# Expert tiles in Strassen pairs: 92 of 128 before the spread, and the gates stored from ScalarE's queue

## The chip, the cores and the metric

The program runs on one core of one Trainium2 chip. The time is device microseconds (us) of one execution. The kernel before took 5091.68 us (median of three runs, 5091.26 to 5094.24). The engines are TensorE (PE in the profile; PEld is its weight load), VectorE (DVE), ScalarE (ACT), GpSimd (POOL) and SyncE (SP), which in this kernel only issues transfers.

## The reference, cut to what matters

One decoder layer: token mixers, cross-attention, and a product-key retrieval of experts. Only the last is touched by the change. With 1024 tokens of width 1024, eight heads, and 128 x 128 experts of one neuron each:

```python
def peer_ffn(h, w_pq, sub_keys, u_emb, v_emb):
    q = (h @ w_pq).reshape(b, s, 8, 2, 128)                 # the queries
    sc = jnp.einsum('bshpc,pnc->bshpn', q, sub_keys)
    top_v, top_i = lax.top_k(sc, 16)                        # 16 of 128, twice
    cand = (top_v[..., 0, :, None] + top_v[..., 1, None, :]).reshape(b, s, 8, 256)
    best_v, best_i = lax.top_k(cand, 16)                    # 16 of 256
    expert = i1 * 128 + i2                                  # from top_i and best_i
    gate = jax.nn.softmax(best_v, axis=-1)
    ...                                                     # by blocks of 128 tokens
        a = jnp.einsum('bthkd,btd->bthk', u_emb[e_blk], h_blk)
        act = (jax.nn.gelu(a) * g_blk)
        return jnp.einsum('bthk,bthkd->btd', act, v_emb[e_blk])
```

The kernel does not gather experts. It computes gelu(u · h) for all 16,384 experts and all tokens, spreads the 128 gates of a token over a row of 16,384, and multiplies densely.

## The kernel before, in words

Matrices are multiplied in `three_pass` (L145): each float32 operand is split into a high part, rounded by ScalarE's copy to the fp32r type, and a low part, the remainder, and a product of a 128 x 128 weight chunk with 512 tokens is three matmuls (high·high, high·low, low·high; L149 to L151). A tile is 128 rows of weights: 8 chunks of the width times two halves of 512 tokens times three passes, so 48 matmuls of 512 columns.

The stages follow each other with a barrier of all engines between them: mixers, merge, cross-attention, then

- **select** (`select_phase`, L1412). The normalised input h, [128, 8, 1024], is made on VectorE and split into `hhi` and `hlo`. A loop over the 8 heads computes per head two tiles of queries (`queries`, L1549), their scores against the keys (`scores`, L1562), and six tiles of gelu(u·h) (`Experts1`, L1339): 48 of the 128 expert tiles in all, which give TensorE work while VectorE picks the top 16, twice, of the head before. At the end the selected indices and gates are turned (transposed) on TensorE, copied out, stored to memory (`sel`) and loaded by the next stage.
- **spread** (`spread_phase`, L1750). The remaining 80 expert tiles, and beside them 64 spread steps of 16 tokens each: VectorE makes a one-hot matrix of the first key and one of the second times the gate (L1862, L1871; four instructions of 128x2048 float16 per step, in two buffers), TensorE multiplies them (L1886, 32 matmuls per step), ScalarE copies the four banks to `stage` (L1906). A group of 128 tokens has eight steps and ten tiles: one tile before each step, and two tiles behind the last. `stage` then holds 8 MB, and SyncE stores it as two transfers of 4 MB (L1820), each issued between two of the tile's own transfers: the load of an expert tile (`uraw`, L1371) and the store of a gelu tile (`gelu_u`, L1376). ScalarE begins the next group's first step only when both have landed.
- **expert** multiplies gelu and gates and runs the second expert matrix, 128 tiles of it, then the final norm.

What one engine does for a tile: SyncE loads 512 KB; ScalarE makes the high part (L1383), GpSimd the low part (L1387); TensorE runs the 48 matmuls; ScalarE applies gelu from each of two banks (L1404); SyncE stores. TensorE waits in `product` for the gelu of the tile before in the same bank. The order on every engine is the order in the code; nothing is reordered.

Of the kernel before, what the change touches and what calls it, by code (L numbers as in the profile page):

```python
# [23 lines left out]
SELECT_TILES = 48  # L24
SB_HD = 64
XH = 4
PH = 8
# [16 lines left out]
class Phase:  # L44
# [9 lines left out]
    def sb(self, name, shape, dt=F32):  # L54
        return self.tensors.enter_context(self.nc.sbuf_tensor(f"{self.tag}_{name}", shape, dt))

# [1282 lines left out]
class Experts1:  # L1339
# [8 lines left out]
    def __init__(self, nc, tensors):  # L1348
        sb = lambda name, shape, dt=F32: tensors.enter_context(nc.sbuf_tensor(name, shape, dt))
        self.nc = nc  # L1350
        self.hhi, self.hlo = sb("hhi", [P, NC, T], F32R), sb("hlo", [P, NC, T], F32R)
        self.raw = sb("uraw", [P, 2, NC, P])
        self.hi, self.lo = sb("uhi", [P, 2, NC, P], F32R), sb("ulo", [P, 2, NC, P], F32R)
        self.out = sb("ugelu", [P, 2, T])

    def begin(self, m, u_stream, a_out):

        self.u_stream, self.a_out = u_stream, a_out
        self.ps = m.ps("a", [P, 2, H])
        self.loaded = [m.sem(f"u_loaded{s}") for s in range(2)]  # L1360
        self.hi_made, self.lo_made = m.sem("uhi_made"), m.sem("ulo_made")
        self.done = m.sem("a_done")
        self.gelu = m.sem("a_gelu", start=2)
        self.stored = [m.sem(f"a_stored{s}", start=1) for s in range(2)]
# [3 lines left out]
    def load(self, sync, tile0, n, slot, first=False):  # L1368
        if not first:
            sync.wait_ge(self.lo_made, n - 1)  # L1370
        sync.dma_start(self.raw[:, slot], self.u_stream[ds(n + tile0, 1)].rearrange("a p c n -> (a p) c n")  # L1371
                       ).then_inc(self.loaded[slot], 16)

    def store(self, sync, tile0, n, slot):
        sync.wait_ge(self.gelu, n * 2 + 4)
        sync.dma_start(self.a_out[ds(n + tile0, 1)].rearrange("a p t -> (a p) t"), self.out[:, slot]  # L1376
                       ).then_inc(self.stored[slot], 16)

    def split_high(self, act, n, m, slot, first=False):
        act.wait_ge(self.loaded[slot], m * 16 + 16)  # L1380
        if not first:
            act.wait_ge(self.done, n * 2 - 2)
        self.nc.scalar.activation(self.hi[:, slot], self.raw[:, slot], ACT.Copy).then_inc(self.hi_made, 1)  # L1383

    def split_low(self, pool, n, slot):
        pool.wait_ge(self.hi_made, n + 1)
        self.nc.gpsimd.tensor_tensor(self.lo[:, slot], self.raw[:, slot], self.hi[:, slot].bitcast(F32), ALU.subtract  # L1387
                                     ).then_inc(self.lo_made, 1)

    def product(self, pe, n, slot):  # L1390
        pe.wait_ge(self.hi_made, n + 1)
        pe.wait_ge(self.lo_made, n + 1)
        for h in range(2):
            pe.wait_ge(self.gelu, n * 2 + (h + 1))
            mm = three_pass(self.nc, self.ps[:, h], [(self.hi[:, slot, k], self.lo[:, slot, k],
                                                      self.hhi[:, k, h * H:h * H + H], self.hlo[:, k, h * H:h * H + H])
                                                     for k in range(NC)])
            mm.then_inc(self.done, 1)

    def activate(self, act, n, m, slot):  # L1400
        act.wait_ge(self.stored[slot], m * 16 + 1)
        for h in range(2):
            act.wait_ge(self.done, n * 2 + (h + 1))
            self.nc.scalar.activation(self.out[:, slot, h * H:h * H + H], self.ps[:, h], ACT.Gelu_apprx_tanh  # L1404
                                      ).then_inc(self.gelu, 1)

    def finish(self, sync, n):
        for s in range(2):
            sync.wait_ge(self.stored[s], n // 2 * 16 + 1)


def select_phase(nc, ex, x_in, gain, keysT, wstream, u_stream, a_out, sel_out):  # L1412


# [4 lines left out]
    with Phase(nc, "select") as m:  # L1419
        K = TOPK  # L1420
        xT = m.sb("xT", [P, NC, T])

        room = xT[:].rearrange("p c t -> p (c t)")
        sc = room[:, 0:2048].rearrange("p (c t n) -> p c t n", c=2, t=NT)
        sc2 = room[:, 2048:4096].rearrange("p (c t n) -> p c t n", c=2, t=NT)
        cand = room[:, 4096:6144].rearrange("p (t n) -> p t n", t=NT)
        cand2 = room[:, 6144:8192].rearrange("p (t n) -> p t n", t=NT)
        sq = ex.out
        norm = Rsqrt(m, "norm", T)
# [3 lines left out]
        w_raw = m.sb("wraw", [P, 2, NC, P])  # L1433
        w_hi, w_lo = m.sb("whi", [P, 2, NC, P], F32R), m.sb("wlo", [P, 2, NC, P], F32R)
        qT = m.sb("qT", [P, 2, T])
# [8 lines left out]
        hit = m.sb("hit", [P, NT, K, K])  # L1444
# [3 lines left out]
        res = m.sb("res", [P, 3, NT, PH, K])  # L1448
        resT = room[:, 0:3 * T].rearrange("p (r t) -> p r t", r=3)

        gemm = m.ps("gemm", [P, 2, H])
        scps = m.ps("scps", [P, 2, NT, KEYS])

# [3 lines left out]
        squares = SumSquares(m, sq, norm.inv, gemm)  # L1457
        h_made, hhi_made, hlo_made = m.sem("h_made"), m.sem("hhi_made"), m.sem("hlo_made")
        w_loaded = [m.sem(f"w_loaded{c}") for c in range(2)]
        whi_made, wlo_made = m.sem("whi_made"), m.sem("wlo_made")  # L1460
        group_done = m.sem("group_done")
        evicted = [m.sem(f"evicted{b}") for b in range(2)]
        scored = m.sem("scored", start=1)
        sc_made = m.sem("sc_made", start=1)
# [10 lines left out]
        turn_done, turn_read = m.sem("turn_done"), m.sem("turn_read")  # L1475
        held = m.sem("held")
        stored = m.sem("stored")
        ex.begin(m, u_stream, a_out)
        NX = SELECT_TILES // PH
        block = m.block()  # L1480

# [6 lines left out]

        @block.sync
        def _(sync):  # L1490
            for i in range(4):
                sync.dma_start(xT[:, 2 * i:2 * i + 2, :], x_in[:, 2 * i:2 * i + 2, :]).then_inc(x_loaded[i], 16)
            sync.dma_start(g_sb[:], gain).then_inc(c_loaded, 16)
            sync.dma_start(keys[:], keysT).then_inc(c_loaded, 16)
            for c in range(2):
                sync.dma_start(w_raw[:, c], wstream[c]).then_inc(w_loaded[c], 16)
            for s in range(2):
                ex.load(sync, 0, s, s, first=True)

            def body(hd, first, last):  # L1500
                for i in range(NX):
                    if i in (0, 1) and not last:
                        sync.wait_ge(wlo_made, hd * 2 + (i + 1))
                        sync.dma_start(w_raw[:, i], wstream[ds(hd * 2 + (2 + i), 1)].rearrange("a p c n -> (a p) c n")
                                       ).then_inc(w_loaded[i], 16)
                    if not (last and i >= NX - 2):
# [244 lines left out]

# [491 lines left out]
```

## Time and profile before

| | |
|---|---|
| median of three runs | 5091.68 us |
| the profiled execution, whole | 5093.29 us |
| its span, first to last instruction | 5091.6 us |
| PE busy | 4756.0 us, 93% |
| DVE, ACT, POOL busy | 2591.5, 1628.5, 1247.9 us |
| mean granted clock of TensorE | 0.962 |

The sum of the prediction is made against the profiled execution, which is 1.6 us above the median. A matmul's own duration in the rows (0.39 us for 512 columns) overlaps the next one's; the pace is read from the distance between starts. Granted clock 1.0 is 2.4 GHz, 0.5 is 1.2 GHz. DMA instructions stand under SPq (or ACTq): their duration is the time the queue's engine spent on issuing, not the transfer.

### The profile page before, as it was taken

The page shows a single profiled execution, that of the slowest core. Times are in us where ns is not written, and L with a number is a line of the kernel's source. Part 1 is how long each engine was busy: PE and PEld are TensorE (multiplying, and loading weights), DVE is VectorE, ACT ScalarE, POOL GpSimd, SP SyncE. Part 2 cuts the span into 40 slices and gives each one's busy share as a digit, 9 for nine tenths or more (in the row PEclk, how much of TensorE's full clock was granted, in tenths as well). Part 3 has the DMA queues.
Part 4 walks back from the last instruction along what each step waited for, and adds up shares of the span by engine and source line. Part 5 has one row for each costly group of instructions (what it writes and reads, how often), then busy time and mean ns, then how long its engine had stood idle before and what let it go on. Part 6 is the DMA issues. An engine that isn't in the chain of part 4 may idle for free. (4 is left out here: it accounts for less than half of the span.)

```text
span 5091.6 us, 64130 instructions
## 1 busy us (share of the span) xinstructions
PE 4756.0 (93%) x22416; PEld 3785.5 (74%) x22416; DVE 2591.5 (51%) x4079; ACT 1628.5 (32%) x2585; POOL 1247.9 (25%) x754
## 2 busy tenths in 40 slices
PE   6999999976988979999989999999799999999998
PEld 5666666644767758888868888888588888888886
DVE  3777777784514235646554444444344444444445
ACT  3555555553413322222223333333211111111111
POOL 1444434431114112212212111211122222222221
PEclk8999999978989979999999999999899999999999
DMA  2111111104432122222224444444644444344341
GB/s 76 38 42 47 46 47 46 38 17 157 153 120 83 56 102 79 83 74 86 79 84 156 148 148 151 154 148 148 227 165 148 144 148 141 138 144 148 140 148 67
DMA packets 260924, 555.78 MB, mean 109 GB/s; under 512 B 15664, under 2 KB 146992, under 8 KB 258608
## 3 DMA queue, kind: packets, MB, share of 16 engines
q1 hardware_dynamic: 260784, 554.01, 31.9%
q8 instruction: 76, 1.25, 0.1%
q14 instruction: 64, 0.52, 0.0%
HBM read 384.60 MB, written 169.35 MB: 109 GB/s over the span
## 5 line engine op out<-in xcount | busy, mean ns | idle before, releaser
L149 PE MATMUL expert_o<-expert_ahi,expert_vhi 128*128 128x512 f32 x2048 | 798.9, 390 | 35.0 <-POOL expert_vlo L2007 30.1
L151 PE MATMUL expert_o<-expert_ahi,expert_vlo 128*128 128x512 f32 x2048 | 797.9, 390 | 0.0
L150 PE MATMUL expert_o<-expert_alo,expert_vhi 128*128 128x512 f32 x2048 | 797.9, 390 | 0.0
L2071 DVE TENSOR_TENSOR expert_acc<-expert_acc,expert_o 128x512 f32<-128x512 f32 x496 | 341.1, 688 | 710.2 <-PE expert_o L151 705.5
L1387 POOL TENSOR_TENSOR ulo<-uraw,uhi 128x1024 fp32r<-128x1024 f32 x128 | 311.7, 2436 | 1373.6 <-ACT uhi L1383 1373.6
L2007 POOL TENSOR_TENSOR expert_vlo<-expert_vraw,expert_vhi 128x1024 fp32r<-128x1024 f32 x128 | 323.1, 2525 | 1053.1 <-ACT expert_vhi L2025 1053.1
L149 PE MATMUL spread_a<-hhi,uhi 128*128 128x512 f32 x1280 | 505.5, 395 | 15.1 <-POOL ulo L1387 15.1
L151 PE MATMUL spread_a<-hhi,ulo 128*128 128x512 f32 x1280 | 499.5, 390 | 0.0
L150 PE MATMUL spread_a<-hlo,uhi 128*128 128x512 f32 x1280 | 498.6, 390 | 0.0
L149 PEld LDWEIGHTS expert_o<-expert_ahi,expert_vhi 128*128 128x128 f32 x2048 | 385.1, 188 | 117.2 <-issue 36.4
L1862 DVE TENSOR_TENSOR spread_one<-spread_iota,spread_parts 128x2048 f16<-128x2048 f16 x64 | 184.0, 2875 | 527.5 <-PE spread_g L1886 526.8
L150 PEld LDWEIGHTS expert_o<-expert_alo,expert_vhi 128*128 128x128 f32 x2048 | 385.2, 188 | 80.1 <-issue 0.2
L151 PEld LDWEIGHTS expert_o<-expert_ahi,expert_vlo 128*128 128x128 f32 x2048 | 385.1, 188 | 80.2
L149 PE MATMUL mix_gemm<-mix_hhi,mix_w_hi 128*128 128x512 f32 x896 | 374.6, 418 | 20.5 <-POOL mix_w_lo L179 13.5
L2031 ACT ACTIVATE expert_ahi<-expert_act 128x1024 fp32r<-128x1024 f32 x128 | 135.8, 1061 | 738.7 <-DVE expert_act L2061 732.1
L550 DVE SCALAR_TENSOR_TENSOR mix_room<-mix_u,mix_cwj,mix_room 128x1024 f32<-128x1024 f32 x240 | 361.3, 1506 | 6.1 <-DVE mix_u L522 3.2
L150 PE MATMUL mix_gemm<-mix_hlo,mix_w_hi 128*128 128x512 f32 x896 | 363.5, 406 | 0.0
L151 PE MATMUL mix_gemm<-mix_hhi,mix_w_lo 128*128 128x512 f32 x896 | 363.0, 405 | 0.0
L149 PE MATMUL select_a<-hhi,uhi 128*128 128x512 f32 x768 | 299.5, 390 | 0.0
L151 PE MATMUL select_a<-hhi,ulo 128*128 128x512 f32 x768 | 298.9, 389 | 0.0
L150 PE MATMUL select_a<-hlo,uhi 128*128 128x512 f32 x768 | 298.8, 389 | 0.0
L1404 ACT ACTIVATE ugelu<-spread_a 128x512 f32<-128x512 f32 x160 | 95.8, 599 | 616.8 <-PE spread_a L151 616.8
(289 smaller groups left out, 8596.9 us busy)
## 6 DMA issues: line engine op xcount, KB each, us to landing
uraw<-in_peer_u SPq DMA_DIRECT2D x128, 512.0 KB, 4.1
gelu_u<-ugelu SPq DMA_DIRECT2D x128, 512.0 KB, 2.9
gates<-spread_stage SPq DMA_DIRECT2D x16, 4096.0 KB, 17.3
expert_act<-gelu_u SPq DMA_DIRECT2D x128, 512.0 KB, 3.6
expert_graw<-gates SPq DMA_DIRECT2D x128, 512.0 KB, 4.4
expert_vraw<-in_peer_v SPq DMA_DIRECT2D x128, 512.0 KB, 6.6
mix_w_raw<-in_w_mix SPq DMA_DIRECT2D x56, 512.0 KB, 3.7
xattn_w_raw<-in_w_cross SPq DMA_DIRECT2D x32, 512.0 KB, 3.6
```

What stands on the lines that cost most here:

```text
L149: nc.tensor.matmul(out, whi, xhi, start=(first and i == 0), stop=False)
L150: nc.tensor.matmul(out, whi, xlo, start=False, stop=False)
L151: mm = nc.tensor.matmul(out, wlo, xhi, start=False, stop=(last and i == len(terms) - 1))
L550: nc.vector.scalar_tensor_tensor(out=ybuf[:, par], in0=u[:, par, t:t + T], scalar=cwj[:, t:t + 1], in1=ybuf[:, par], op0=ALU.mult, op1=ALU ...
L1387: self.nc.gpsimd.tensor_tensor(self.lo[:, slot], self.raw[:, slot], self.hi[:, slot].bitcast(F32), ALU.subtract).then_inc(self.lo_made, 1)
L1404: self.nc.scalar.activation(self.out[:, slot, h * H:h * H + H], self.ps[:, h], ACT.Gelu_apprx_tanh).then_inc(self.gelu, 1)
L1862: return nc.vector.tensor_tensor(pairwise(dst), keys, twice(row, n), ALU.is_equal)
L2007: return eng.tensor_tensor(low, raw, high.bitcast(F32), ALU.subtract)
L2031: nc.scalar.activation(ahi[:, par, e], act[:, e], ACT.Copy).then_inc(ahi_made, 1)
L2071: nc.vector.tensor_tensor(acc[:, k, h * H:h * H + H], acc[:, k, h * H:h * H + H], ops[:, d, h], ALU.add).then_inc(added, 1)
```

## The change

In the stages before select, and in expert, nothing is changed but line numbers (moved by six in the shared helpers).

**Pairs.** In select, two tiles go together as a pair (256 rows x 1024 of the width, times 1024 tokens), cut into 2 x 2 blocks on every side, and are multiplied by Strassen's scheme in Winograd's form: seven products of half size instead of eight. A half product is 4 chunks x 3 passes = 12 matmuls of 512 columns, a pair 84. The eight query pairs and 46 pairs of expert tiles (92 tiles) make 54 pairs. GpSimd makes four sums of 128x512 per pair (L1414 on) and the low parts of seven blocks; ScalarE the high parts; the token side's sums T are made once, by VectorE, when the stage begins. The products come out in four banks; ScalarE copies the first one, VectorE adds the others in seven instructions of 128x512 into the buffer `out`, and ScalarE applies gelu there, in place.

```diff
+    def sums(self, pool, n, m, s):
+        a, g = self.raw[:, s], self.nc.gpsimd
+        pool.wait_ge(self.loaded[s], m * 16 + 16)
+        g.tensor_tensor(a[:, 2], a[:, 0], a[:, 2], ALU.subtract).then_inc(self.sum_made, 1)
+            pool.wait_ge(self.done, n * self.NP - 4)
+        g.tensor_tensor(self.s2[:], a[:, 3], a[:, 2], ALU.subtract).then_inc(self.sum_made, 1)
+        g.tensor_tensor(self.s14[:, s, 0], a[:, 0], self.s2[:], ALU.add).then_inc(self.sum_made, 1)
+        g.tensor_tensor(self.s14[:, s, 1], a[:, 1], self.s2[:], ALU.subtract).then_inc(self.sum_made, 1)
...
+    def product(self, pe, n, s, j, made=None):
+        if j != 1:
+            pe.wait_ge(self.lo_made, n * 4 + (group + 1))
+        if j == 0 and not first:
+            pe.wait_ge(self.added, n * self.NP - 3)
+        if j == 1 and not first:
+            pe.wait_ge(self.added, n * self.NP - 1)
+        if j == 2 and not first:
+            pe.wait_ge(self.added, n * self.NP)
...
+            mm = three_pass(self.nc, self.ps[:, bank], [(high[:, kp], low[:, kp], b_hi[:, k], b_lo[:, k])],
```

**Select's VectorE work.** The top-16 search of a head was one block. It is cut into pieces of one to eight instructions that stand between the additions of six pairs. The turned indices go straight from the banks into `parts` (kept in the shared buffer `front`), so `sel` is neither stored nor loaded, and the turning is done inside the last five pairs. On VectorE, third pair of a head, where the old `select_xT<-select_top` is the candidate sum (L1700) and the new one `front<-select_top` (L1888); `front<-front,select_products` are the pair's additions. Before:

```order
L1697 MAX_INDEX select_idx<-select_top,select_xT 128x8 x16
L1700 TENSOR_TENSOR select_xT<-select_top 128x256 x8
L1705 CAST select_idxf<-select_idx 128x256
L1709 MAX select_best<-select_xT 128x8 x8
L1712 MAX_INDEX select_bidx<-select_best,select_xT 128x8
```

After:

```order
L1884 MAX_INDEX select_idx<-select_top,front 128x8 x2
L1888 TENSOR_TENSOR front<-select_top 128x256 x3
L1490 TENSOR_TENSOR front<-front,select_products 128x512
L1492 TENSOR_TENSOR front<-front,select_products 128x512
L1888 TENSOR_TENSOR front<-select_top 128x256 x5
L1495 TENSOR_TENSOR front<-front,select_products 128x512
L1979 CAST select_idxf<-select_idx 128x256
```

The eight candidate sums now stand three before and five behind a pair's additions, and the addition at L1495, for which TensorE's next pair waits, stands behind the five.

**Spread.** 36 tiles are left. A group of 128 tokens has four tiles (the last has eight): six half tiles, then the eight steps, with one half tile behind the second and one behind the fourth step; the last group's other eight half tiles come last. VectorE's step buffers are three instead of two. Gelu's output buffer and its stores are by half tile (256 KB). The loops are written out.

```diff
+        def order(tt, half, step):
+            first, between, rest = halves(tt)
+            for n, h in first:
+                half(n, h)
+            for st in range(0, STEPS, 2):
+                step(tt * STEPS + st)
+                step(tt * STEPS + st + 1)
+                for n, h in between[st // 2:st // 2 + 1]:
+                    half(n, h)
...
+    def product(self, pe, n, h):
+        pe.wait_ge(self.lo_made, n + 1)
+        if n:
+            pe.wait_ge(self.gelu, 2 * n + h - 1)
...
+                if n >= 3:
+                    dve.wait_ge(g_done, (n - 2) * NB)
...
-                part = slice(i * KEYS // NS, (i + 1) * KEYS // NS)
-                sync.dma_start(g_out[part].rearrange("a p t -> p a t")[:, :, ds(tt * P, P)], stage[:, part, :]
-                               ).then_inc(stored, 16)
+                if st == STEPS - 1:
+                    act.wait_ge(staged, (n + 1) * NB)
+                    for i in range(NS):
+                        part = slice(i * KEYS // NS, (i + 1) * KEYS // NS)
+                        nc.scalar.dma_start(g_out[part].rearrange("a p t -> p a t")[:, :, tt * P:tt * P + P], stage[:, part, :]
+                                             ).then_inc(stored, 16)
```

`NS` goes from 2 to 4. The store of the gates leaves SyncE's queue. There it stood, behind the eighth step of a group, between a tile's load and store:

```order
L1371 DMA uraw<-in_peer_u 128x1024
L1818 ISA
L1820 ISA
L1820 DMA gates<-spread_stage 128x64x128
L1375 ISA
L1376 ISA
L1376 DMA gelu_u<-ugelu 128x1024
```

It is now on ScalarE, at the end of a group's steps (`spread_stage<-spread_g` are the copies out of the banks, four per step):

```order
L2235 ACTIVATE spread_stage<-spread_g 128x128x4 x8
L2098 ACTIVATE spread_ugelu<-spread_a 128x512
L2078 ACTIVATE spread_uhi<-spread_uraw 128x1024
L2235 ACTIVATE spread_stage<-spread_g 128x128x4 x16
L2241 DMA gates<-spread_stage 128x32x128 x4
L2098 ACTIVATE spread_ugelu<-spread_a 128x512 x2
L2078 ACTIVATE spread_uhi<-spread_uraw 128x1024
```

Four issues of 2 MB each stand ahead of the gelu of the next group's first tile, in ScalarE's own order.

## Rows read from the trace of the kernel before

**Rows 1.** Stages, by window: us, then busy time and count by engine, clock, DMA share, GB/s.
```profile
core 0: us, PE busy (x) PEld busy (x) DVE busy (x) ACT busy (x) POOL busy (x), PEclk, DMA share, GB/s
1878.00:1912.00 34.00, 29.81 (x96) 20.89 (x97) 15.20 (x13) 10.03 (x11) 4.83 (x2) 0.73 0.05 16
1912.00:2623.00 711.00, 708.18 (x3234) 587.36 (x3232) 419.13 (x1711) 170.04 (x225) 146.57 (x60) 1.00 0.23 78
2623.00:2643.40 20.40, 4.84 (x24) 3.81 (x24) 0.29 (x1) 5.70 (x8) 2.81 (x3) 0.59 0.50 197
2643.40:3640.00 996.60, 994.14 (x5888) 829.10 (x5888) 412.14 (x257) 335.88 (x525) 190.80 (x79) 1.00 0.47 147
3640.00:3669.50 29.50, 0.03 (x1) 0.06 (x1) 7.23 (x5) 3.10 (x4) 2.64 (x2) 0.56 0.90 313
```

**Rows 2.** ACT's timeline in select: start, us, instruction, idle before and releaser.
```profile
2233.34 0.60 ACT L1404 ACTIVATE ugelu<-select_a 128x512 f32<-128x512 f32 x1 [4.84 <-PE select_a L151]
...
2244.22 0.60 ACT L1404 ACTIVATE ugelu<-select_a 128x512 f32<-128x512 f32 x1 [4.84 <-PE select_a L151]
```

**Rows 3.** Groups by line and shape, POOL: busy us, mean ns, idle before.
```profile
L1387 POOL TENSOR_TENSOR ulo<-uraw,uhi 128x1024 fp32r<-128x1024 f32 x128 | 311.7, 2436 | 1373.6 <-ACT uhi L1383 1373.6
...
L327 POOL TENSOR_TENSOR mix_sp_lo<-mix_softplus,mix_sp_hi 128x512 fp32r<-128x512 f32 x48 | 61.7, 1285 | 219.8 <-ACT mix_sp_hi L473 218.2
```

**Rows 4.** Timeline of DVE, POOL and PE around the first spread steps.
```profile
2653.15 1.23 DVE L1862 TENSOR_TENSOR spread_one<-spread_iota,spread_parts 128x2048 f16<-128x2048 f16 x1 [0.62 <-DVE spread_parts L1847]
...
2657.93 1.22 DVE L1862 TENSOR_TENSOR spread_one<-spread_iota,spread_parts 128x2048 f16<-128x2048 f16 x1
2657.95 3.45 POOL L1387 TENSOR_TENSOR ulo<-uraw,uhi 128x1024 fp32r<-128x1024 f32 x1 [12.46 <-ACT uhi L1383]
2658.15 1.96 PE L1886 MATMUL spread_g<-spread_gate,spread_one 128*128 128x128 f16 x32 [1.85 <-DVE spread_gate L1871]
...
2659.07 3.42 DVE L1862 TENSOR_TENSOR spread_eq<-spread_iota,spread_parts 128x2048 f16<-128x2048 f16 x1
```

**Rows 5.** Timeline of DVE and POOL at the end of a head in select.
```profile
2061.19 2.29 DVE L1739 TENSOR_TENSOR select_hit<-select_hit,select_idxf 128x2048 f32<-128x2048 f32 x1
2063.28 2.46 POOL L1387 TENSOR_TENSOR ulo<-uraw,uhi 128x1024 fp32r<-128x1024 f32 x1 [8.47 <-ACT uhi L1383]
2063.61 2.29 DVE L1742 TENSOR_REDUCE select_res<-select_hit 128x2048 f32 x1
```

**Rows 6.** One line, expert's additions out of a bank: duration ns, min/median/max.
```profile
L2071 DVE TENSOR_TENSOR expert_acc<-expert_acc,expert_o x496: 675/689/689, 3682.7 to 5027.1; 128x512 f32<-128x512 f32 x166
```

**Rows 7.** SyncE's timeline behind the first group of steps.
```profile
2751.45 0.41 SPq L1820 DMA_DIRECT2D gates<-spread_stage  x1
2761.36 3.34 SPq L1376 DMA_DIRECT2D gelu_u<-ugelu  x1
...
2766.16 1.08 SPq L1820 DMA_DIRECT2D gates<-spread_stage  x1
2772.23 9.36 SPq L1376 DMA_DIRECT2D gelu_u<-ugelu  x1
```

**Rows 8.** The 16 stores of L1820, each 4 MB: issue to landing.
```profile
DMA to landing us min/median/max: 16.0/17.3/19.0
```

**Rows 9.** SyncE's timeline at the end of spread.
```profile
3640.07 8.05 SPq L1376 DMA_DIRECT2D gelu_u<-ugelu  x1
3654.26 0.35 SPq L1981 DMA_DIRECT2D expert_act<-gelu_u  x1
```

**Rows 10.** SyncE's timeline from the end of cross-attention to select.
```profile
1842.17 0.32 SPq L1064 DMA_DIRECT2D x<-xattn_xq  x1
1846.74 2.05 SPq L1492 DMA_DIRECT2D select_xT<-x  x4
```

**Rows 11.** Timeline of SyncE and PE where spread begins.
```profile
2636.07 0.81 SPq L1371 DMA_DIRECT2D uraw<-in_peer_u  x2
...
2643.41 0.79 PE L149 MATMUL spread_a<-hhi,uhi 128*128 128x512 f32 x1 [15.11 <-POOL ulo L1387]
...
2647.25 0.39 PE L149 MATMUL spread_a<-hhi,uhi 128*128 128x512 f32 x1
```

More of the change, by code:

```diff
@@ L1336, in _ @@
                         nc.vector.tensor_tensor(x, x, gemm[:, h], ALU.add).then_inc(bank_read, 1)
[L1339 to L1409, printed above, removed]
@@ L1652, in _ @@
             dve.wait_ge(squares.done, 1)
[L1653 removed]
+            norm.start(nc, dve, [(slice(h * H, h * H + H), pr.ps[:, h]) for h in range(2)], lambda h: sum_read[h])
             norm.finish(nc, dve)
@@ new lines, in spread_phase, with halves @@
+        g_done = m.sem("g_done")
+        staged = m.sem("staged")
+        stored = m.sem("stored")
+        block = m.block()
+        def halves(tt):
+            count = PER if tt < NT - 1 else TILES - PER * (NT - 1)
+            every = [(tt * PER + i // 2, i % 2) for i in range(2 * count)]
+            return every[:FIRST], every[FIRST:FIRST + BETWEEN], every[FIRST + BETWEEN:]
+        def order(tt, half, step):
[7 more added lines that the diff above has]
+                    half(n, h)
+            for n, h in rest:
+                half(n, h)
@@ L1824, in _ @@
-            tiles(sync, step, extra)
-            ex.finish(sync, KEYS - SELECT_TILES)
-            sync.wait_ge(stored, 16 * NS * NT + 1)
+            for n in range(3):
+                ex.load(sync, n)
+            for n in range(TILES):
+                ex.store(sync, SELECT_TILES, n, 0)
+                if n + 3 < TILES:
+                    ex.load(sync, n + 3)
+                ex.store(sync, SELECT_TILES, n, 1)
+            for h in range(2):
+                sync.wait_ge(ex.stored[h], 16 * TILES)
@@ L1885, in step @@
                         for i in range(2):
-                            mm = nc.tensor.matmul(ps[:, bank, x], one1[:, b, t], gate[:, i, b, t], start=(i == 0), stop=(i == 1))
+                            mm = nc.tensor.matmul(ps[:, bank, x], one1[:, b, t], gate[b][:, i, t], start=(i == 0), stop=(i == 1))
                     mm.then_inc(g_done, 1)
-            tiles(pe, step, lambda i, tt, tile, half, b, left: ex.product(pe, tile, b))
+            for tt in range(NT):
+                order(tt, lambda n, h: ex.product(pe, n, h), step)
@@ L1917, in expert_phase @@
+            for tt in range(NT):
+                order(tt, half, step)
 def expert_phase(nc, a_in, x_in, g_in, v_stream, final_gain, out):
```

813 lines of the change are left out of this document (552 added, 261 removed).

## The prediction

> **What bounds the kernel now.** I read the page's busy shares first: PE is busy 93% of the span, no other engine over 51%. Then the windows by stage [rows 1]: in select's steady part PE is busy 708 of 711 us and in spread 994 of 997, both at granted clock 1.00 (2.4 GHz). The time of these stages is the number of matmuls, so a change that takes matmuls away is paid in full as long as nothing else becomes late. The pace comes from ScalarE's timeline: two gelus of the same bank start 10.88 us apart [rows 2], a tile of 48 matmuls, so 0.2267 us per matmul and 5.44 us per half tile. A spread step's 32 matmuls take 1.96 us [rows 4]; as a check, 80 tiles at 10.88 and 64 steps at 1.96 are 996 us [rows 1]. What stands outside: PE idles or crawls for 34 us at select's first tiles, 20 us between select and spread, 29.5 us before expert [rows 1].
>
> **Matmuls removed.** Select and spread have 16 query and 128 expert tiles, 144 x 48 = 6912 matmuls. After: 54 pairs x 84 + 36 x 48 = 6264. 648 fewer, x 0.2267 = **-147 us**. Steps and scores stay.
>
> I follow the new kernel on the clock of the profiled execution.
>
> **Select begins (to 1932).** The first products wait for h as before (1878). Before, the first query pair was through at 1912 [rows 1]. Now products 3 to 6 of the first pair wait for the token sums T: four sums and four low parts of 128x2048 on VectorE, 2.3 us each (as L1739, [rows 5]), 18.6 us behind h. GpSimd, which was idle then, makes sums and low parts at the same time, and where both engines read two operands from SBUF the later one waits for the other's whole instruction: the POOL instruction at 2657.95 took 3.45 instead of 2.4 us (the DVE instruction in flight ended at 2659.1), and the DVE instruction at 2659.07 took 3.42 instead of 1.22, of which 2.3 until POOL's end at 2661.4 [rows 4]. I count five or six such collisions, about 7 us before h is ready and 3 behind. First pair done at about 1932.
>
> **Select runs (to 2988).** A pair is 84 x 0.2267 = 19.04 us on PE. Per pair GpSimd has five instructions of 128x512 (1.285 us) and three of 128x1024 (2.44) [rows 3]: 13.7 us, so it keeps up. VectorE has 419/8 = 52 us of selection per head [rows 1] plus 42 additions of 0.62 to 0.69 us [rows 6]: 80 us in a head's 118, so it keeps up on average too. What can make PE wait is a late addition. PE's third product needs the last addition of the pair before, two products (5.4 us) after its source was done. Laying a head's pieces between the additions with the rows' durations, this slack is used up at one place: the five candidate sums that stand ahead of the third pair's last addition read two SBUF operands while GpSimd works on the next pair; they alternate with its instructions and the addition comes about 1.4 us late. The four 2.3 us instructions of the last pair lose time in the same way, but fit. The reduction does not collide: it began at 2063.61 inside a POOL instruction and took its 2.29 [rows 5]; nor do the additions, with one operand in a bank: 675 to 689 ns through the whole of expert [rows 6]. So 8 x 1.4 = 11 us (bounds 0 and 50: no piece late, or every pair late by about 1). Select's last matmul: 1932 + 53 x 19.04 + 30 for the scores (unchanged) + 5 for turning (4.84, [rows 1]) + 11 = 2988. Before it ended at 2620.
>
> **Select to spread (to 3002).** Before 23 us, with turning, store and reload of the selection. Now the last addition and gelu (1.5 us), a store; from such a store's issue to the next stage's first instruction it is 4.6 us [rows 10], and from that to the first product 7.3 [rows 11]. 14 us.
>
> **Spread.** Work: 36 x 10.88 + 64 x 1.96 = 517 us. Two waits are new.
>
> VectorE: a step costs it 4.8 us (2653.15 to 2657.93, [rows 4]) against PE's 1.96. Before, a tile stood between two steps. Now steps 5 to 8 of a group follow each other, and three are buffered ahead. The fourth is begun when the first is multiplied, and so on; with one half tile behind the second and one behind the fourth step, steps 7 and 8 each come 3 us late (one GpSimd collision among them). **+6 per group, +48**; and 0.6 per group where ScalarE's copies of consecutive steps (4 x 0.51) outlast PE's 1.96: +5. Bounds: 20 and 70.
>
> ScalarE's queue: this is the term that decides. On SyncE, a transfer issued behind 4 MB of 512-byte runs is held: the 4 MB issue itself took 0.41 us, but the next transfer, tried 9.9 us later, was held 3.34 us, until 13.3 us behind the big issue; behind the second it was held 9.36 us, until 15.4 us behind it [rows 7]. The store lands after 16.0 to 19.0 us [rows 8]. So an issue is accepted only when nearly all runs of the one before have been handed on, some 3 us before it lands. SyncE had nothing else to do; ScalarE has. Four issues of 2 MB at the same 290 GB/s (4 MB in 14 us): the second is accepted after about 6, the third 7 later, the fourth 7 later. ScalarE is held about **20 us** and gives no gelu. PE gets through the first tile of the next group (two half tiles, 10.9 us) and then waits for that tile's first gelu. It started 0.9 us before ScalarE's issues, so it waits 0.9 + 20 + 0.5 + 0.6 - 10.9 = 11 us. That is 8 times, as the last group has tiles behind it too: +89. An idle time of this length lowers the clock: behind the 15 us at 2643.41, nine matmuls took 3.84 us instead of 2.04 [rows 11], so +1.7 each, +14. Together **+103**. Bounds: 0, if ScalarE's issues go through at 0.4 us each; and 150, if each is held as long as half of SyncE's second case and the loads on the other queue share the rate (26 us).
>
> Spread ends at 3002 + 517 + 53 + 103 = 3675.
>
> **Before expert.** The gates' last store was issued at 3632 and ended the stage: from the last gelu store at 3640.07 to expert's first transfer were 14.2 us, 8.05 of them held [rows 9]. Now eight half tiles stand behind it, so only the 4.6 us of a barrier [rows 10] are left, and expert starts 5.3 us behind the last product: 3681, against 3654.26. From there nothing changes. +27 us on 5093.3 is 5120; against the median, **5119 us**, 0.5% slower. The sum again: -147 matmuls, +23 first pair (20 late, less the 3 already counted for its product), +11, -9 and -10 between stages, +53, +103 and +3 of rounding.
>
> By the Trainium skill (DMA: Bandwidth & Descriptors, "Issuing engines are not separate DMA queues") issuing from several engines saves only the sequencer's time for the issue, "which is usually small relative to the DMA itself". Taken at its word, the four issues cost ScalarE little, and the time would be that of the first rival below. The held issues of SyncE in this trace speak against it for runs this short.
>
> **Rivals.**
> 1. *ScalarE is not held.* Its queue takes all four issues at 0.4 us, as SyncE's first did. For it: each store is half as large, and that queue carries nothing else. Against: SyncE's third transfer was small and still waited, so it isn't the waiting transfer's size. The +103 goes: **5016 us**, faster. The half tiles ahead of the steps (32.6 us) cover the landing of 8 MB (about 30), so nothing takes its place. Chance 0.22.
> 2. *Held half as long.* Two stores of 2 MB are taken like one of 4: held 13 us, PE waits 3 to 4, clock stays up: 103 - 28 = 75 less: **5044 us**. Against it: the queue was still closed 13.3 of some 17 us behind the issue, when most of the 4 MB had gone. Chance 0.08.
> 3. *VectorE and GpSimd lose more in select.* If collisions delay every pair by about a microsecond instead of one in six, +40 on top of my forecast: **5160 us**, slower. It decides from the point where additions come more than 5.4 us behind their product. For it: GpSimd's share of busy time rises from 21% to 70%, which no row shows beside this VectorE load. Against: the additions themselves do not collide. Chance 0.08.
>
> **How the numbers follow.** My forecast has 0.62; its own range is 5090 to 5150, from 17 to 24 us of holding (8 us of time per us held) and 10 either way for the rest. Over all cases 8 in 10 lie in 5010 to 5155. A measurement here can tell 0.2%, 10 us, from no change: faster (below 5081) is rivals 1 and 2 and a tail of mine, 0.33; same 0.11; slower 0.56.
>
> **What would show it.** Right: ACTq rows of the gates' store with one short and three of 5 to 8 us, eight times; PE waiting about 11 us for gelu at the start of the third half tile of each group, with the clock at 0.5 behind it; PE waiting 3 us for the gates in the seventh and eighth step; spread's first product near 3002 and last near 3675; PE busy all but some 10 us between 1932 and 2988. Wrong: short ACTq rows (rival 1), or waits on the additions in every pair (rival 3). If GpSimd's low parts, not the additions, are what PE waits for in select, my account of the pair is wrong.

## The result and the profile after

The changed kernel takes 5106.57 us (median of 12 runs, 5101.93 to 5110.31), the kernel before 5095.51 (12 runs beside it, 5091.26 to 5099.69): ratio 1.0022 [1.0013, 1.0031]. It is slower, as forecast, by 11 us instead of 27. The profiled execution has a span of 5100.3 us against 5091.6.

PE ran 21768 matmuls against 22416: the 648 are gone. Stages of the changed kernel by window, columns as in [rows 1]:

```profile
1876.00:1921.40 45.40, 28.66 (x85) 19.36 (x85) 42.02 (x28) 18.52 (x18) 21.11 (x9) 0.64 0.13 47
1921.40:2971.30 1049.90, 1044.70 (x4733) 867.70 (x4731) 740.95 (x2086) 378.42 (x493) 760.77 (x419) 1.00 0.28 98
2971.30:2984.50 13.20, 0.04 (x2) 0.03 (x1) 8.51 (x7) 2.74 (x3) 2.81 (x3) 0.58 0.47 160
2984.50:3659.50 675.00, 542.75 (x3776) 455.53 (x3776) 333.16 (x252) 202.06 (x362) 83.86 (x35) 0.91 0.53 153
3659.50:3678.10 18.60, 0.00 (x0) 0.00 (x0) 7.18 (x5) 3.24 (x4) 2.63 (x2) 0.59 0.80 312
```

The first row is the first pair, the second the rest of select, the fourth spread. Select is full, with VectorE at 71% and GpSimd at 72%. Spread is not: PE is busy 543 of 675 us, where it was busy 994 of 997 [rows 1]. PE's waits there, from the table of waits (us in total, times, longest; the last row is PE waiting for ScalarE's copies out of the banks):

```profile
PE spread_a L155 <- ACT spread_ugelu L2098: 89.4, 8, 11.3
PE spread_g L2213 <- DVE front L2199: 25.1, 11, 2.8
PE spread_g L2213 <- DVE spread_gate L2199: 10.8, 5, 2.8
PE spread_g L2213 <- ACT spread_stage L2235: 6.5, 16, 0.4
```

Behind the first group of steps, ScalarE's queue, ScalarE and PE (start, duration; the bracket is the idle time before and its releaser):

```profile
3053.02 20.60 ACTq L2241 DMA_DIRECT2D gates<-spread_stage  x4
3073.73 1.08 ACT L2098 ACTIVATE spread_ugelu<-spread_a 128x512 f32<-128x512 f32 x2 [20.73 <-issue]
3074.47 0.76 PE L155 MATMUL spread_a<-h_hi,spread_uhi 128*128 128x512 f32 x1 [11.28 <-ACT spread_ugelu L2098]
```

ScalarE is held 20.6 us by four issues, and does both gelus of the tile together only then. PE waits 11.28 us, eight times over the stage. The clock around it, in windows of 5 us (last three columns: granted clock, DMA share, GB/s):

```profile
3063.00:3068.00 5.00, 0.19 (x1) 0.00 (x0) 1.55 (x2) 0.00 (x0) 0.00 (x0) 0.76 1.02 285
3068.00:3073.00 5.00, 0.00 (x0) 0.00 (x0) 0.00 (x0) 0.00 (x0) 0.00 (x0) 0.50 1.02 291
3073.00:3078.00 5.00, 3.53 (x8) 2.81 (x9) 0.00 (x0) 2.03 (x3) 2.17 (x1) 0.50 1.02 287
3078.00:3083.00 5.00, 5.00 (x21) 4.06 (x20) 0.00 (x0) 0.55 (x1) 0.20 (x1) 0.88 1.01 313
```

It falls to 0.50 (1.2 GHz) while PE stands, and stays there for some microseconds of work.

The two other places of which the prediction speaks. The first pair:

```profile
1890.63 2.45 POOL L1415 TENSOR_TENSOR select_raw_low<-select_raw,select_hi 128x1024 fp32r<-128x1024 f32 x1 [7.86 <-ACT select_hi L1426]
1890.89 4.33 DVE L1845 TENSOR_TENSOR front<-front 128x2048 f32<-128x2048 f32 x1
1904.53 0.79 PE L155 MATMUL select_products<-select_t_hi,select_hi 128*128 128x512 f32 x1 [11.90 <-DVE select_t_lo L1842]
```

The collision is there (2.3 us of work took 4.33: VectorE stood until GpSimd's end at 1893.08 and then took its own length), but it is the only one of this size on the path between h and the third product at 1904.53. Later ones fall beside PE's work. And the third pair of a head:

```profile
2341.38 1.76 DVE L1888 TENSOR_TENSOR front<-select_top 128x256 f32<-128x256 f32 x5
2342.03 1.05 ACT L1426 ACTIVATE select_hi<-select_s 128x1024 fp32r<-128x1024 f32 x1
2343.06 0.68 DVE L1495 TENSOR_TENSOR front<-front,select_products 128x512 f32<-128x512 f32 x1
2343.15 2.41 POOL L1415 TENSOR_TENSOR select_s_low<-select_s,select_hi 128x1024 fp32r<-128x1024 f32 x1 [3.51 <-ACT select_hi L1426]
```

The five candidate sums took 1.76 us, not delayed, because GpSimd stood idle 3.51 us: its last low part waited for ScalarE's high part, which in ScalarE's order stands behind the gelu of a block that VectorE had just finished. PE waited 1.0 us for an addition, once and inside the first pair; in the rest of the stage it waited for none.

### The profile page after: what moved, and what is told of

Its sections match the earlier page's. It is cut to its first block and busy times, and to the rows that moved or that the text cites. A ratio compares the mean times of both kernels' runs of the same rounds, so it can differ in the third digit from the quotient of the medians.

```text
span 5100.3 us, 62049 instructions
## 1 busy us (share of the span) xinstructions
PE 4633.1 (91%) x21768; PEld 3688.1 (72%) x21768; DVE 2872.7 (56%) x4467; ACT 1706.3 (33%) x2690; POOL 1772.2 (35%) x1078
## 5 line engine op out<-in xcount | busy, mean ns | idle before, releaser
L155 PE MATMUL select_products<-h_hi,select_hi 128*128 128x512 f32 x864 | 339.1, 393 | 16.1 <-DVE h_lo L1828 12.8
L156 PE MATMUL select_products<-h_lo,select_hi 128*128 128x512 f32 x864 | 338.0, 391 | 0.0
L155 PE MATMUL spread_a<-h_hi,spread_uhi 128*128 128x512 f32 x576 | 236.5, 411 | 102.6 <-ACT spread_ugelu L2098 89.4
L2187 DVE TENSOR_TENSOR front<-spread_iota,front 128x2048 f16<-128x2048 f16 x107 | 147.4, 1411 | 282.4 <-PE spread_g L2213 277.8
L2082 POOL TENSOR_TENSOR spread_ulo<-spread_uraw,spread_uhi 128x1024 fp32r<-128x1024 f32 x36 | 86.4, 2402 | 577.6 <-ACT spread_uhi L2078 577.6
L1415 POOL TENSOR_TENSOR select_raw_low<-select_raw,select_hi 128x1024 fp32r<-128x1024 f32 x108 | 278.5, 2579 | 15.5 <-ACT select_hi L1426 11.4
L155 PE MATMUL select_products<-select_t_hi,select_hi 128*128 128x512 f32 x648 | 253.9, 392 | 15.9 <-DVE select_t_lo L1842 11.9
L2356 ACT ACTIVATE expert_vhi<-expert_vraw 128x1024 fp32r<-128x1024 f32 x128 | 134.8, 1054 | 384.9 <-PE expert_o L157 382.5
L1415 POOL TENSOR_TENSOR select_s_low<-select_s,select_hi 128x512 fp32r<-128x512 f32 x108 | 219.2, 2030 | 114.0 <-ACT select_hi L1426 114.0
```

The lines of the kernel that those rows point to most:

```text
L155: nc.tensor.matmul(out, whi, xhi, start=(first and i == 0), stop=False)
L156: nc.tensor.matmul(out, whi, xlo, start=False, stop=False)
L1415: self.nc.gpsimd.tensor_tensor(low, src, high.bitcast(F32), ALU.subtract).then_inc(self.lo_made, 1)
L2082: self.nc.gpsimd.tensor_tensor(self.lo[:, n % 3], self.raw[:, n % 3], self.hi[:, n % 2].bitcast(F32), ALU.subtract).then_inc(self.lo_made, 1)
L2187: return nc.vector.tensor_tensor(pairwise(dst), keys, twice(row, n), ALU.is_equal)
L2356: nc.scalar.activation(vhi[:, q], vraw[:, q], ACT.Copy).then_inc(vhi_made, 1)
```

## The experiments

Theory A, at the outset: the four issues hold ScalarE, and its late gelu is what stops TensorE. Each ratio below is to the kernel before, run beside it on the same chip.

**One and two issues.** The same 8 MB of a group, on the same queue:

```diff
-        NS = 4
+        NS = 1          # and 2 in the second run
```

> The gates of a group go out as one store of 8 MB on ScalarE's queue instead of four of 2 MB; nothing else differs from the changed kernel. Theory A (an issue is held while the runs of the issue before it are handed on, and costs 0.4 us when nothing is ahead of it): one ACTq row of about 0.4 us per group, no wait of PE for gelu at the start of a group (89 us gone) and no low clock behind it (some 20 us gone), so about 110 us less than the changed kernel: near 4995 us, ratio to the kernel before 0.981. Rival B (ScalarE is held for as long as the bytes take, however they are cut): ACTq held about 20 us, no change, ratio 1.002. Rival C (it is the 8 MB of writes that slow the loads and gelu stores of the first tiles, whoever issues them): PE's wait stays, ratio 1.00.

Measured: 5029.51 us, ratio 0.9872 [0.9857, 0.9887]. Rivals B and C, under which nothing changes, fall.

> Two stores of 4 MB per group on ScalarE's queue. Theory A: the second issue is held some 13 us, as on SyncE before (13.3 us from issue to acceptance), ScalarE about 14 us in all; PE waits 0.9 + 14 + 1.1 - 10.9 = 5 us per group instead of 11.3, so 50 us less from the wait and up to 10 from the clock: 5045 to 5057 us, ratio 0.990 to 0.992. Rival B: held 20 us as before, ratio 1.002. If the queue takes 4 MB in advance without holding, the time is that of one issue.

Measured: 5049.79 us, 0.9909 [0.9894, 0.9924]. ScalarE's queue was held 13.19 us behind the first group, and PE waited 29.5 us for gelu in all. The ratio is in the expected range by two misses: a wait was 3.7 us and not 5, but the clock gave nothing back (the table in the next section). With one issue, the line of the store, and PE's waits:

```profile
L2241 ACTq DMA_DIRECT2D gates<-spread_stage x8: 378/378/434, 3059.2 to 3543.1; - x8
DMA to landing us min/median/max: 34.9/36.9/37.8
...
PE spread_g L2213 <- ACT spread_stage L2235: 28.0, 16, 4.7
PE spread_g L2213 <- DVE front L2199: 21.5, 7, 3.5
PE spread_g L2213 <- DVE spread_gate L2199: 6.5, 2, 3.2
```

An issue of 8 MB costs ScalarE 0.38 us, no more than one of 2 MB; the wait of 89.4 us is gone. So the hold is shown: it is the issue *behind* an unfinished one that waits. Of some 108 us expected (1.0022 to 0.981), 76 came. The 8 MB land 36.9 us behind the issue, and the work that PE has meanwhile (the cover: six half tiles) is 32.6. ScalarE can't copy the first step of a group before the landing, so the banks stay full and PE stands at the second step, up to 4.7 us; the 28.0 us of the row hold some 4 us of ordinary copies. With four issues this wait was hidden behind the gelu's. While the 8 MB are under way the DMA engines are full, with the gates and the tiles' own transfers together (a window of the same run; last three columns: clock, DMA share, GB/s):

```profile
3138.00:3160.00 22.00, 22.00 (x120) 18.30 (x119) 0.00 (x0) 4.53 (x7) 4.78 (x2) 1.00 1.06 325
```

**The same four issues on SyncE's queue,** between the first tiles' transfers:

```diff
+            def gates(tt, i):
+                sync.wait_ge(staged, (tt + 1) * STEPS * NB)
+                sync.dma_start(g_out[part]..., stage[:, part, :]).then_inc(stored, 16)
```

> The same four stores of 2 MB, but on SyncE's queue, issued between the transfers of the next group's first tile: one ahead of its first gelu store, one behind it, two behind its second. Theory A: SyncE is held instead, up to 8 us at an issue; PE's wait of 89 us for gelu goes, with the low clock, but gelu stores land late, and a gelu two tiles on may wait for its buffer up to 3 us per group: 85 to 110 us less than the changed kernel, 4997 to 5022 us, ratio 0.981 to 0.986. Rival C (the writes themselves delay the tiles): most of the wait stays, ratio about 1.00.

Measured: 5052.6 us, 0.9916 [0.9901, 0.9931]: less gain than expected. PE's direct waits for gelu fell to 3.0 us, once, but at the second step of a group it waited up to 6.5 us for ScalarE's copies, 44.4 us in all. That is not the landing. Behind the second group, SyncE's queue and ScalarE:

```profile
3144.59 8.20 SPq L2160 DMA_DIRECT2D gates<-spread_stage  x2
3152.83 7.28 SPq L2072 DMA_DIRECT2D gelu_u<-spread_ugelu  x1
3164.22 0.60 ACT L2098 ACTIVATE spread_ugelu<-spread_a 128x512 f32<-128x512 f32 x1 [11.39 <-DMA gelu_u<-spread_ugelu]
3168.60 3.23 ACT L2252 ACTIVATE spread_stage<-spread_g 128x512 f32<-128x512 f32 x6
```

SyncE, held by the gates' last two issues, stores the gelus late, and ScalarE waits for a free gelu buffer: 15 times, up to 12.1 us, 110.6 in all. The gates had landed at 3163.49; ScalarE's first copy comes at 3168.60, behind the late gelus. Theory A had named this wait, with 3 us per group. With the stores on SyncE the kernel is 41 us faster than before; with the same four issues on ScalarE it takes 54 us more than that.

**Why the additions were not late.** ScalarE's last high part stands ahead of block 3's gelu:

```diff
-                    pr.activate(act, n, 3)
                 if more:
                     pr.high(act, n + 1, m_next, s_next, 3)
+                if kind is None:
+                    pr.activate(act, n, 3)
```

> In select, ScalarE makes the last high part of the next pair ahead of the third block's gelu instead of behind it, so that GpSimd's last low part does not wait for an addition; nothing else. My reading of why the 11 us of late additions did not come: at the candidate sums this order keeps GpSimd's last low part away until the sums are through. If so, it now starts about 1.5 us earlier there, collides with the sums, the third pair's last addition comes up to 2.4 us later, and PE waits at most 1.5 us per head: 0 to 12 us more than the changed kernel. Rival: the additions have 2 us to spare whatever the order is, and nothing changes (within 3 us).

Measured: 5120.76 us, 1.0049 [1.0036, 1.0063], some 14 us more than the changed kernel. Its table of waits has a row that the changed kernel's has not:

```profile
PE select_products L155 <- DVE front L1495: 12.4, 8, 1.6
```

Eight times up to 1.6 us, where the prediction had eight times 1.4. The 64 candidate sums (L1888) took a mean of 1202 ns, against 790 in the changed kernel. The predicted collision is real; it was missing because GpSimd was late itself. PE's waits in spread stayed within 2 us of the changed kernel's, so the time is lost in select.

**How many half tiles stand ahead of the steps** (with one issue):

```diff
-        FIRST, BETWEEN = 6, 2
+        FIRST, BETWEEN = 5, 3          # and 7, 1
```

> One 8 MB store per group, as in the run with one issue (0.9872 of before; there the first step of a group waited 4.7 us for its landing, 28 us in all, and steps 7 and 8 waited 28 us for VectorE). Here five half tiles stand ahead of the steps and three among them. Theory A (the store lands about 37 us behind its issue whatever TensorE does, and VectorE's work on a step is fixed at about 4.8 us): 5.4 us less of cover, so the landing wait rises to about 10 us in seven or eight groups (+38 to +43), and the extra half tile among the steps takes all of VectorE's 28 us; sum +10 to +15, ratio 0.989 to 0.990. Theory B (TensorE's halves slow the transfers, so that the landing wait does not grow by as much as the cover shrinks): ratio 0.983 to 0.987, faster than the run with one issue.

Measured: 5035.65 us, 0.9883 [0.9867, 0.99]. VectorE's waits went from 28.0 to nothing, the landing's from 28.0 to 70.1: +42, as theory A had it (+38 to +43). It still landed after 36.0 us. The time rose by 6 us only, and not by 10 to 15: PE's slow pace behind waits became less (table in the next section).

> The other side: seven half tiles ahead of the steps, one among them, one 8 MB store. Theory A: the landing wait goes (28 us less), VectorE's waits grow by 5.4 us per group (+43), and the longer idle time costs clock; sum +15 to +22, ratio 0.990 to 0.992. Theory B (VectorE uses the longer lead to be further ahead): it can't, three sets are the limit, but if the waits for VectorE were mostly from collisions with GpSimd and those move away, ratio below 0.987.

Measured: 5028.12 us, 0.9867 [0.985, 0.9883]. The landing wait went (28.0 to 3.3), VectorE's grew to 54.3, by 26 and not by 43. So the trade is even between 6 and 7, and my sum was too dear. Part of VectorE's waits with six was not a lack of time but a collision, as the next run shows.

**Where the two half tiles stand among the steps** (with one issue): behind the fourth and sixth step.

```diff
-                for n, h in between[st // 2:st // 2 + 1]:
+                for n, h in between[st // 2 - 1:st // 2] if st else ():
```

> One 8 MB store, six half tiles ahead and two among the steps, but behind the fourth and sixth step instead of the second and fourth. Theory A (what VectorE has ready when the eighth step is due sets the sum of a group's waits, wherever the halves stand ahead of it): the same time as the run with one issue, ratio 0.986 to 0.989, with the waits moved from steps 7 and 8 to steps 4 to 6. Theory B (each wait arises locally, at the steps that follow each other without a half tile between): more or less than that by 10 us or more.

Measured: 5010.08 us (5005.15 to 5012.43), **0.9834 [0.9817, 0.985]**, the fastest version. Theory A's "same time" was wrong. PE's waits:

```profile
PE spread_g L2213 <- ACT spread_stage L2235: 34.0, 13, 6.1
PE spread_g L2213 <- DVE front L2197: 5.8, 1, 5.8
PE spread_g L2213 <- DVE front L2199: 2.6, 1, 2.6
```

VectorE's fell from 28.0 to 9.5 by the table, and to 3.7 in truth: the single 5.8 us stands at a second step, where six other groups wait 4.1 to 6.1 us for the landing, and VectorE's operands for that step had been ready 33 us before. So the landing's waits are 39.8, up from 28.0. The same group in both timelines, first with the half tiles behind steps 2 and 4:

```profile
3114.44 3.19 POOL L2082 TENSOR_TENSOR spread_ulo<-spread_uraw,spread_uhi 128x1024 fp32r<-128x1024 f32 x1 [18.14 <-ACT spread_uhi L2078]
3115.33 4.52 DVE L2187 TENSOR_TENSOR front<-spread_iota,front 128x2048 f16<-128x2048 f16 x2
3122.43 3.42 PE L2213 MATMUL spread_g<-front 128*128 128x128 f16 x32 [3.48 <-DVE front L2199]
```

then behind 4 and 6:

```profile
3118.47 2.97 POOL L2082 TENSOR_TENSOR spread_ulo<-spread_uraw,spread_uhi 128x1024 fp32r<-128x1024 f32 x1 [28.33 <-ACT spread_uhi L2078]
3119.02 1.99 PE L2213 MATMUL spread_g<-front 128*128 128x128 f16 x32 [0.41 <-ACT spread_stage L2235]
3119.23 3.29 DVE L2197 TENSOR_TENSOR front<-front 128x2048 f16<-128x2048 f16 x1
```

GpSimd's low part of the next tile follows the second half tile and collides with VectorE in both. In the first it meets VectorE's work for the eighth step, which took 7.0 us instead of 4.9; that step is due at once and PE waits 3.48 us. In the second it meets the work for the next group's first step, which PE starts 30 us after it is ready; the eighth step's was ready 2.1 us early.

**VectorE's share of a step** (with one issue; the multiplication of the gates' low part is left out):

```diff
                 nc.vector.tensor_tensor(high, low, twice(2, n), ALU.mult)
-                nc.vector.tensor_tensor(low, low, twice(3, n), ALU.mult)
```

> One 8 MB store, and VectorE's multiplication of the low part of the gates is left out (the low half then holds ones instead of the gate's remainder), so that a step costs VectorE 3.6 us instead of 4.8. It prices VectorE's waits and the clock that they cost. Theory A: the 28 us of waits for the gates and their dips of the clock in steps 6 to 8 go together, 28 + 10 to 15 us; but the steps then end earlier while the store still takes 37 us from its issue, and this cover is unchanged, so nothing takes their place: ratio 0.979 to 0.981. Theory B (the clock falls because of the landing wait at the head of a group, not because of VectorE): 28 us only, ratio 0.982, and dips to 0.85 stay.

Measured: 5011.51 us, 0.9834 [0.9817, 0.985]. VectorE's waits 12.4 us, the landing's 35.7: 8 us less waiting together, for 18 us of time. Neither theory had the landing's wait grow, from 28.0 to 35.7; about half of the gain is not waits but PE's pace behind them. The gain is about that of the later half tiles, which leave nothing out.

**The later half tiles alone, on the changed kernel** (four issues, the same line moved):

```diff
-                for n, h in between[st // 2:st // 2 + 1]:
+                for n, h in between[st // 2 - 1:st // 2] if st else ():
```

> The changed kernel as it is, with its four 2 MB issues on ScalarE's queue; alone the two half tiles among the steps stand behind the fourth and sixth step instead of the second and fourth. Theory A (the two new waits of spread are separate: TensorE's 89 us for the gelu behind the held issues stay, VectorE's 36 us fall to about 12, with some clock): 20 to 30 us less than the changed kernel, ratio to before 0.996 to 0.998. Theory B (the time that VectorE gives back goes into the held issues or the landing): ratio 1.001 to 1.003.

Measured: 5103.18 us (10 runs), 1.0018 [1.0008, 1.0027], not separable from the changed kernel's 1.0022. Theory A had 20 to 30 us.

```profile
PE spread_a L155 <- ACT spread_ugelu L2098: 93.5, 8, 11.8
PE spread_g L2213 <- DVE front L2199: 13.2, 5, 2.6
PE spread_g L2213 <- DVE spread_gate L2199: 8.2, 4, 2.6
...
3099.22 2.36 POOL L2082 TENSOR_TENSOR spread_ulo<-spread_uraw,spread_uhi 128x1024 fp32r<-128x1024 f32 x1 [8.49 <-ACT spread_uhi L2078]
3099.41 3.26 DVE L2187 TENSOR_TENSOR front<-spread_iota,front 128x2048 f16<-128x2048 f16 x1 [34.79 <-PE spread_g L2213]
3106.38 0.93 PE L2213 MATMUL spread_g<-spread_gate,front 128*128 128x128 f16 x7 [2.65 <-DVE spread_gate L2199]
...
3103.00:3108.00 5.00, 2.35 (x29) 2.14 (x27) 4.93 (x5) 2.56 (x6) 0.00 (x0) 0.77 0.00 0
```

VectorE's waits fell by 14.5 us, and the gelu waits rose by 4. In every group the fourth step now waits 2.6 us: its buffer comes free only when the first step is multiplied, four steps follow each other, and GpSimd's low part of the tile collides with VectorE's first instruction for it (3.26 us instead of 1.22). The clock falls there, to 0.77 in the window shown, and the slow pace takes back what the waits gave (table in the next section). The run with one issue and later half tiles has the same four steps in a row. Its first group, which has no store ahead of it, also waits 2.6 us at the fourth step; the other seven stand 4.1 to 6.1 us at the second step, for the landing, and not at the fourth, since VectorE catches up meanwhile. So the later half tiles pay with one issue partly because the landing's wait covers the fourth step. That the collision, and not the row of four alone, makes the 2.6 us was not tested by itself.

**Two queues.** Half tiles behind 4 and 6; 4 MB from ScalarE's queue and 4 MB from SyncE's, then 6 and 2:

```diff
+                    sync.dma_start(g_out[CUT:KEYS]..., stage[:, CUT:KEYS, :]).then_inc(stored, 16)
...
+                    nc.scalar.dma_start(g_out[0:CUT]..., stage[:, 0:CUT, :]).then_inc(stored, 16)
```

> Half tiles behind the fourth and sixth step, and the 8 MB of a group as one issue of 4 MB on ScalarE's queue and one of 4 MB on SyncE's, ahead of the next tile's stores. The run with one issue and the later half tiles took 0.9834 of before, with 34 us of waits for the landing (37.8 us behind the issue, against 32.6 of cover). Theory A (the 8 MB go through at what one queue gives; two run beside each other): landing at 30 us or less, the 34 us go, ratio 0.976 to 0.979, unless SyncE, held behind its 4 MB, stores a gelu late, for which TensorE would then wait. Theory B (16 DMA engines or the memory set the rate of 512-byte runs, whichever queue they come from): landing stays at 35 to 38 us, and SyncE's held stores add gelu waits of 5 to 10 us per group: ratio 0.985 to 1.00.

Measured: 5105.02 us, 1.0019 [1.001, 1.0029]. The issues (KB each, median us to landing), SyncE behind its issue, PE's wait and ScalarE's:

```profile
gates<-spread_stage SPq DMA_DIRECT2D x8, 4096.0 KB, 29.9
gates<-spread_stage ACTq DMA_DIRECT2D x8, 4096.0 KB, 34.7
...
3053.44 0.39 SPq L2163 DMA_DIRECT2D gates<-spread_stage  x1
3058.32 18.65 SPq L2072 DMA_DIRECT2D gelu_u<-spread_ugelu  x1
...
PE spread_a L155 <- ACT spread_ugelu L2098: 92.4, 8, 11.6
...
ACT spread_ugelu L2098 <- DMA gelu_u<-spread_ugelu: 181.1, 16, 20.2
```

4 MB alone landed after 16.0 to 19.0 us [rows 8]; two at once take 29.9 and 34.7. That is hardly sooner than 8 MB in one issue (37.8), and no sooner than the changed kernel's four issues from one queue, the last of which landed 33.3 to 35.6 us behind the first, with the tiles' transfers held there too. The rate is shared; theory B. And SyncE, held 18.65 us with the gelu's store, keeps the gelu buffer full: ScalarE waits for the buffer (last row), PE for ScalarE. The hold came back by another way, at the same price.

> As the run before with 6 MB on ScalarE's queue and 2 MB on SyncE's. Theory A: landing of the 6 MB at some 28 us, SyncE held under 8 us, which the gelu buffers cover: ratio 0.976 to 0.979. Theory B: landing 35 to 38 us, and no gelu wait, since SyncE is held less: ratio 0.983 to 0.985.

Measured: 5017.41 us, 0.9848 [0.9832, 0.9865]: theory B again. The 6 MB land after 39.1 us, PE waits 50.4 us for the landing and not for gelu.

## Why the prediction was right in direction and wrong in size

The forecast was 27 us more than before, and 11 were measured. The step that failed is the term for late additions in select, +11 us for five candidate sums that collide with GpSimd: the runs show no such wait, because GpSimd's low part itself waits for ScalarE. The first pair's collisions were sized too dear beside it. Positions in the profiled execution, us:

| | predicted | measured | difference |
|---|---|---|---|
| first pair done | 1932 | 1921.4 | -11 |
| select's last product | 2988 | 2971.3 | -17 |
| spread's first product | 3002 | 2984.5 | -17 |
| spread's last product ends | 3675 | 3659.1 | -16 |
| expert's first transfer | 3681 | 3663.1 | -18 |

- **Matmuls removed, -147.** Right: 648 fewer, at clock 1.00 in select.
- **First pair, +23: too dear by 7,** beside 3 us that the stages before, not changed, took less (select's first transfer at 1843.54 instead of 1846.74 [rows 10]). I summed collisions wherever VectorE met them; one of 2 us lay on the path to the third product, and PE was busy behind it. That it was a matter of the path is read from the timeline, not tried.
- **Late additions, +11: the step that failed.** Measured nothing in the part of select to which it belongs. I let GpSimd take its next instruction as soon as it was free, but its last low part waits for ScalarE. With ScalarE's order turned, the term appears with its predicted place, count and size (12.4 us, 8 times): shown by that run. Small waits at the scores, which I had not counted (3.0 and 2.0 us in the table of waits), took some 5 us of it back, so the rest of select came 6 us sooner than forecast.
- **Select to spread and before expert.** 13.2 us for 14, and 4.0 for 5.3.
- **VectorE's waits in spread, +48: measured 35.9;** ScalarE's copies +5: 6.5. The rule (three sets ahead, 4.8 us each) is borne out by the three splits of the half tiles, which trade one wait for the other. One collision with GpSimd is a good part of the waits at the seventh and eighth step (2 us of VectorE's work for one step); the later half tiles move it to where it costs nothing.
- **ScalarE held, +89: measured 89.4,** with 20.6 us for the 20 predicted, and removed by one issue. But I let 32.6 us of half tiles cover a landing of about 30; it took 35 to 39, so even rival 1 would have missed its 5016 us (one issue took 5029.51). The rival of issues that cost ScalarE nothing falls: 0.38 us is all that an issue costs on an empty queue, up to 7.67 behind a full one. The Trainium skill (DMA: Bandwidth & Descriptors, "Issuing engines are not separate DMA queues") calls the time of an issue small beside the transfer's; this case agrees for the first issue and not for the ones behind it, and agrees with the section's heading in the two-queue runs.
- **Low clock, +14: too cheap.** Each half tile behind a gelu wait took 7.8 to 7.9 us instead of 5.44, so 2.4 us were lost eight times, 19 us, where I had 1.7. Spread's 674.6 us less the 517 of work and 132 of waits leave 26 in all; 3 more of them lie in the stage's first half tile. This made up for VectorE's 12 less, and spread's total (673 forecast) was right by two errors of opposite sign, which is luck.

Spread in six of the runs, us: from the first product to the last, PE's waits, and what is left above the 517 of work, the slow pace:

| | length | waits | left |
|---|---|---|---|
| changed kernel, four issues | 674.6 | 131.8 | 26 |
| two issues | 618.4 | 67.7 | 34 |
| one issue | 595.4 | 56.0 | 22 |
| one issue, five half tiles ahead | 600.8 | 70.1 | 14 |
| one issue, later half tiles | 572.8 | 43.5 | 12 |
| four issues, later half tiles | 672.7 | 121.5 | 34 |

The slow pace doesn't go with the length of the waits, and taking away the gelu waits, with the landing's in their place, gave back 3 us of it, not the 20 that I expected of one issue.

So the direction rests on the one term that was right, ScalarE held. Of the 18 us of error about 13 are two terms in select, both collisions that I counted without asking who else was waiting; 3 are the stages before, and 2 the turns between stages. The second rival, held half as long, is near what two issues made (5049.79 us for 5044), though the clock did not stay up as it had it. The third, slower additions in every pair, did not occur.

## What to carry to other kernels

A large transfer is issued in one piece if its engine has anything else to do: what holds an engine is not the size of a transfer but the issue behind an unfinished one. Before moving a transfer off one queue, look who stands behind it on the new one, and what late result each of those would make; when such a wait is removed, expect the landing itself to be next (here 28 to 40 us, where 89 had gone). A collision between two engines costs time only where the delayed one is due. Moving two half tiles, so that one collision met work that was due 30 us later, was worth 19 us here, but only beside one issue: with four, the same move laid bare another wait and gained nothing that could be measured. A table of waits names the last event before a wait ends; look at the timeline before the name is believed (the copies that waited for a gelu buffer, and the 5.8 us above).

## What the runs showed of the hardware that was not expected

- An issue of 8 MB in 512-byte runs occupied ScalarE's queue for 0.378 us, one of 2 MB on an empty queue as long; four of 2 MB held it 20.6 us, two of 4 MB 13.2.
- 8 MB in such runs took 35 to 39 us to land as one issue beside the tiles' transfers, with the DMA share at 1.06 and 325 GB/s in all in the window shown; 34.3 to 35.0 from two queues at once and 33.3 to 35.6 as four issues from one queue. A second queue added nothing.
- A half tile of 5.44 us took 7.8 to 7.9 behind waits of 11.1 to 11.3 us, and 7.2 to 8.5 behind waits of 2.8 to 4.2 us (two issues): the shorter wait did not cost less pace.
